# First attention: projection pieces two together in every second unit, in place of one in most units

## The chip, the cores and the metric

The kernel runs on one core of one Trainium2 chip. Time is the device time of one execution in microseconds (us); lower is better. A core has a tensor engine (PE, with its weight loads shown apart as PEld), VectorE (DVE), ScalarE (ACT), GpSimd (POOL) and a sync engine (SP) that here only issues transfers. Each runs its own program in order, and they meet through semaphores. Sixteen DMA engines serve the queues of SP, ACT and POOL.

## The reference

One decoder layer on 512 tokens of width 1024, float32. Two attentions read the same normalised input through one combined projection, their outputs are normalised, joined and projected, and an MLP follows:

```python
h = rms_norm(x, ln1_g[l])
proj = h @ w_in[l]
h_q, h_kv, h_kr, q_b, kv_b, gate_b = jnp.split(proj, offsets, axis=-1)
o_a = mla_mixer(h_q, h_kv, h_kr, ...)      # 8 heads, causal over 512 tokens
o_b = nsa_mixer(q_b, kv_b, gate_b, ...)    # 8 heads, 3 branches: compressed, selected, window
mix = jnp.concatenate([rms_norm(o_a, ...), rms_norm(o_b, ...)], axis=-1)
x = x + mix @ w_o[l]
h2 = rms_norm(x, ln2_g[l])
x = x + jnp.square(jax.nn.relu(h2 @ w_up[l])) @ w_down[l]
```

The change concerns how `kv_b`, the gates and the compressed branch's input (columns of `w_in` that only the second attention needs) are computed while the first attention runs.

## The kernel before

Tokens lie in 4 tiles `t` of 128. Weights are loaded in pieces of 128 x 1024 (`PIECES`) by SP into 3 raw slots. ACT rounds each piece to its high part (`split_hi`), DVE makes the rest (`split_lo`), and every product is made of three matmuls: high by high, low by high, high by low (`three`). A ring of 5 slots holds split pieces. SP issues the load of piece n when piece n - 3 has been split (`raw_free`).

The first attention (`mla`) is the list of the first 32 `UNITS`, one for each tile and head: unit n is tile n // 8, head n % 8. All engines walk through the units in one software pipeline, written out by hand. In step n PE does this, in this order: the scores of unit n; the projection pieces that `unit_of` puts there (`project`); the head transposes of steps 4 and 8 (`turn_heads`); the product with the values for unit n - 4 (from unit 16 on four units together); the transposes of the probabilities of unit n - 2 (`turn_unit`); and the transposes of a row whose norm was begun in step n - 4 (`turn_nsa`). In step n ACT copies out transposes of unit n - 3 (`pt_out`, the other ones are DVE's), makes the exponential of unit n - 1 (`exp_unit`), copies the keys of the second attention (`pair_his`), takes the squares of a row (`norm_in`), takes the gates and raw taps (`compress_in`) and splits weights. In step n DVE does `pt_out`, the mask and the maximum (`low_unit`), `pair_los`, `nsa_turned`, `nsa_row`, `nsa_sum`, `gate_row`, `out_row`, and the low halves of the pieces of step n - 1. POOL makes the powers of -1/2 in between, and issues one accumulating transfer behind each of them (`add_up`). Two PSUM banks each serve projections (`D`), transposes (`T`), scores (`S`) and outputs (`O`); a transpose waits until the one before the last has been copied out (`take`).

`ROWS` has 8 rows of projections for the second attention: `nkv` for tiles 0 to 3 (512 columns: keys and values of two branches), then `cmp` for tiles 0 to 3 (280 columns: compressed branch and gates). Each is 4 pieces of 6 matmuls. `ROW_END`, the step in which a row's last piece stands, sets when all that follows it is done:

```python
NORM_AT = {ROW_END[0]: ("nkv", 0), ROW_END[1]: ("nkv", 1), 9: ("nq", 3), ROW_END[2]: ("nkv", 2), ROW_END[3]: ("nkv", 3),
           16: ("nq", 2), 19: ("nq", 1), 22: ("nq", 0)}
PAIR_KEYS = {ROW_END[4 + t] + 1: t for t in range(NT)}
PAIR_LOWS = {n + int(t < NT - 1): t for n, t in PAIR_KEYS.items()}
```

A row in `NORM_AT` at step m has its squares (ACT) and sum (DVE) in step m + 1, its scaling (`nsa_row`, DVE) in step m + 3, its transposes (PE) in step m + 4 and their copy (`nsa_turned`, DVE) in step m + 5. `nq` rows are the queries of the second attention, whose projections were made earlier. The split of the pieces behind the `nkv` rows stands in steps 13 and 14, and that of output-projection piece `wo` 0 in step 17. The load of `wo` 0 waits for the low half of the second `cmp` piece, made by DVE in step 14.

Of the kernel before, what the change touches and what calls it, by code (L numbers as in the profile page):

```python
# [195 lines left out]


def unit_of(row, piece_):
    return 2 + (4 * row + piece_) * 27 // 32


ROW_END = [unit_of(r, 3) for r in range(len(ROWS))]

NORM_AT = {ROW_END[0]: ("nkv", 0), ROW_END[1]: ("nkv", 1), 9: ("nq", 3), ROW_END[2]: ("nkv", 2), ROW_END[3]: ("nkv", 3),
# [40 lines left out]
for _m, _n in enumerate(SPLITS[RING:]):  # L245
    _g = last_user(SPLITS[_m])
    _what = PIECES[_n][0]
    if _m + RING < BY_NAME:
        continue
    if _what == "wo":  # L250
        SPLIT_AT_UNIT.setdefault(N_MLA + WO_SPLIT[PIECES[_n][1]], []).append(_n)
    elif _g == ("wo", 0, NT - 1, 1):
        SPLIT_AT_UNIT.setdefault(N_MLA + 51, []).append(_n)
    elif _g == ("nkv", NT - 1):
        SPLIT_AT_UNIT.setdefault(1 + unit_of(ROWS.index(_g), PIECES[SPLITS[_m]][1]), []).append(_n)
    else:
        SPLIT_AFTER.setdefault(_g, []).append(_n)
# [76 lines left out]
def build(nc, a, out, known):  # L334
    with ExitStack() as ctx:
# [1793 lines left out]
        def _(pe):  # L2129
# [367 lines left out]
            for n in range(last + 10):  # L2497
# [6 lines left out]
                if n < N_MLA:  # L2504
                    for r, key in enumerate(ROWS):
                        here = [i for i in range(4) if unit_of(r, i) == n]
                        if here:
                            project(*key, here)
# [241 lines left out]
```

How the kernel before makes its waits and increments, by code:

```python
        @block.sync  # L712
# [5 lines left out]
                cols = slice(0 if i else 2 * P, D_MODEL)  # L718
                sp.dma_start(x_t[i][:, cols], a["x_t"][i, :, cols]).then_inc(*xt_in[i, part].mark())
            for n, (what, i, width, split) in enumerate(PIECES):
                for part, at_piece in X_LOADS.items():
                    if at_piece == n:
                        load_turned(*part)
                for t in ROWS_AT.get(n, ()):
                    load_x(t)
                if n >= RAW:
                    sp.wait_ge(*raw_free(n - RAW))
                if what == "quad" and n + 1 - RAW >= PIECE_AT["quad", (0, 0)]:
                    j = PIECES[n - RAW]
                    if j[0] == "quad":
                        sp.wait_ge(*dve_step.at(("w_diff", j[1][1])))
                if what == "sum" and PIECES[n - RAW][0] == "quad":
                    sp.wait_ge(*dve_step.at(("w_diff", PIECES[n - RAW][1][1])))
                if what == "sum":
                    k = SUM_JOBS.index(i)
                    sp.wait_ge(*sum_added[k % 4].at(k))
                    source = sums_dram[k]
                elif what in ("A", "B"):
                    k = 2 * i + int(what == "B")
                    sp.wait_ge(*up_added[k // BATCH].at(BATCH * (k // BATCH) + BATCH - 1))
                    source = up_sums[k]
                else:
                    source = a["w_pairs"][i, 0] if what == "P" else a["w_down"][i[0], i[1]] if what == "quad" else a["weights"][n, :, 0:width]
```

## Time and profile before

| | us |
|---|---|
| median of 3 runs (lowest, highest) | 633.57 (632.98, 635.29) |
| the profiled execution | 635.07 |
| its span in the trace | 633.2 |
| PE busy in the span | 621.1 |
| DVE busy | 499.6 |
| ACT busy | 399.5 |
| first attention, scores of units 0 to 31 | 92.5 to 169.5 |

Times in the trace count from the start of the span. A row of the timeline gives the start, the duration, the engine, the line of the kernel, what is written and read, and in brackets how long the engine was idle before and what released it. Matmuls are pipelined, so starts say more than durations.

### The profile page before, as it was taken

What the parts mean: (1) busy time and instruction counts of PE and PEld (TensorE: products, weight loads), DVE (VectorE), ACT (ScalarE), POOL (GpSimd) and SP (SyncE); (2) the same over time, 40 slices, a digit from 0 to 9 for tenths busy, and PEclk for the clock granted to TensorE, in tenths of its full rate; (3) what the DMA queues carried; (4) which work ended last, traced back from release to release, by engine and by line L of the source; (5) the groups of instructions that cost most, each with busy time, mean ns of one, the idle gap of its engine ahead of it and who ended that gap; (6) DMA issues with size and microseconds to landing.
All of it is one profiled execution on the core that took longest, in us unless ns stands there. A gap on an engine that the chain in (4) does not pass through costs nothing.

```text
span 633.2 us, 11668 instructions
## 1 busy us (share of the span) xinstructions
PE 621.1 (98%) x4105; PEld 550.9 (87%) x4105; DVE 499.6 (79%) x936; ACT 399.5 (63%) x800; POOL 161.0 (25%) x230
## 2 busy tenths in 40 slices
PE   7999999998999999999999999999999999999998
PEld 6999888887788888887899999999998888888886
DVE  6766666579988788897897787777778999998664
ACT  6584775657997647657458667676657464755660
POOL 0655655434332202212110111111111212222200
PEclk8999999999999999999999999999999999999999
DMA  8883528996999955996355878788877899899972
GB/s 325 290 320 129 203 108 325 294 298 184 256 271 295 356 184 171 293 257 145 68 135 184 224 212 226 203 202 234 182 169 168 230 230 251 217 247 283 282 252 100
DMA packets 34793, 142.48 MB, mean 225 GB/s; under 512 B 5319, under 2 KB 5831, under 8 KB 33776
## 3 DMA queue, kind: packets, MB, share of 16 engines
q1 hardware_dynamic: 22832, 83.66, 37.2%
q0 software_dynamic: 10208, 34.88, 30.1%
q10 hardware_dynamic: 1696, 23.21, 9.8%
q8 instruction: 33, 0.54, 0.3%
q14 instruction: 24, 0.20, 0.1%
HBM read 139.57 MB, written 65.06 MB: 323 GB/s over the span
## 4 chain that ended last, share of the span: by engine, by line
PE 89%; DVE 4%; ACT 3%; DMA 2%; issue 1%; POOL 0%; ACTq 0%; DVEq 0%; POOLq 0%
PE bank L2147 15%; PE bank L2149 15%; PE bank L2148 15%; PE bank L2556 7%; PE bank L2555 7%; PE bank L2554 7%; PE bank L2167 7%; PE bank L2392 3%; PE bank L2335 2%; PE bank L2374 2%; DMA raw<-weights 1%; PE bank L2346 1%; PE bank L2347 1%; PE bank L2490 1%; PE bank L2492 1%
## 5 line engine op out<-in xcount | busy, mean ns | idle before, releaser
L881 POOL DMA_DIRECT2D down_sums<-w_down x64 | 49.8, 779 | 229.0 <-PE bank L2556 137.0
L2147 PE MATMUL bank<-w_hi,act_hi 128*128 128x512 f32 (+3 forms) x222 | 88.7, 400 | 0.1
L2148 PE MATMUL bank<-w_lo,act_hi 128*128 128x512 f32 (+3 forms) x222 | 79.7, 359 | 0.0
L2149 PE MATMUL bank<-w_hi,act_lo 128*128 128x512 f32 (+3 forms) x222 | 79.7, 359 | 0.0
L1128 ACT ACTIVATE p_buf<-s_buf,stats 128x128 f32<-128x128 f32 (+3 forms) x96 | 53.8, 561 | 30.4 <-PE bank L2167 16.2
L1420 DVE TENSOR_TENSOR w_lo<-raw,w_hi 128x1024 fp32r<-128x1024 f32 (+1 forms) x50 | 60.0, 1207 | 15.1 <-ACT w_hi L987 14.7
L987 ACT ACTIVATE w_hi<-raw 128x1024 fp32r<-128x1024 f32 (+1 forms) x50 | 51.6, 1040 | 29.5 <-DMA raw<-w_pairs 21.8
L1370 ACT ACTIVATE w_hi<-raw 128x1024 fp32r<-128x1024 f32 x31 | 32.8, 1057 | 35.8 <-DMA raw<-down_sums 20.0
L2147 PE MATMUL bank<-w_hi,s_all 128*128 128x512 f32 x140 | 54.6, 390 | 0.0
L2148 PE MATMUL bank<-w_lo,s_all 128*128 128x512 f32 x140 | 54.5, 389 | 0.0
L2149 PE MATMUL bank<-w_hi,s_all 128*128 128x512 f32 x140 | 54.5, 389 | 0.0
L2147 PEld LDWEIGHTS bank<-w_hi,act_hi 128*128 128x128 f32 x222 | 42.3, 191 | 6.8 <-issue 1.4
L2554 PE MATMUL bank<-g_all,w_hi 128*128 128x256 f32 x168 | 47.5, 283 | 0.0
L2555 PE MATMUL bank<-g_all,w_hi 128*128 128x256 f32 x168 | 47.5, 283 | 0.0
L2556 PE MATMUL bank<-g_all,w_lo 128*128 128x256 f32 x168 | 47.5, 283 | 0.0
L2556 PE MATMUL bank<-act_hi,w_lo 128*128 128x256 f32 x168 | 47.5, 283 | 0.0
L2555 PE MATMUL bank<-act_lo,w_hi 128*128 128x256 f32 x168 | 47.5, 283 | 0.0
L2554 PE MATMUL bank<-act_hi,w_hi 128*128 128x256 f32 x168 | 47.5, 283 | 0.0
L2167 PE MATMUL bank<-consts,p_buf 128*128 128x128 f32 x248 | 45.1, 279 | 2.4 <-ACT pt_buf L1140 1.0
L2148 PEld LDWEIGHTS bank<-w_lo,act_hi 128*128 128x128 f32 x222 | 42.3, 191 | 5.9 <-issue 1.2
L2149 PEld LDWEIGHTS bank<-w_hi,act_lo 128*128 128x128 f32 x222 | 42.3, 190 | 5.4
L2028 DVE TENSOR_TENSOR w_lo<-raw,w_hi 128x1024 fp32r<-128x1024 f32 x31 | 37.8, 1219 | 11.3 <-ACT w_hi L1370 11.1
(329 smaller groups left out, 1832.0 us busy)
## 6 DMA issues: line engine op xcount, KB each, us to landing
down_sums<-w_down ACTq DMA_DIRECT2D x32, 512.0 KB, 6.4
down_sums<-w_down POOLq DMA_DIRECT2D x64, 256.0 KB, 5.7
raw<-down_sums SPq DMA_DIRECT2D x32, 512.0 KB, 4.9
up_sums<-w_pairs POOLq DMA_DIRECT2D x28, 512.0 KB, 9.8
raw<-up_sums SPq DMA_DIRECT2D x28, 512.0 KB, 4.8
raw<-weights SPq DMA_DIRECT2D x26, 512.0 KB, 5.8
up_sums<-w_pairs SPq DMA_DIRECT2D x16, 512.0 KB, 6.3
raw<-w_down SPq DMA_DIRECT2D x16, 512.0 KB, 5.3
```

The costliest lines, as they stand in the source:

```text
L881: pool.dma_start(sums_dram[k, rows_], a["w_down"][SUMS[m][1], step, rows_], accum_op=ALU.add, max_dma_last_dim=4096).then_inc(*sum_added[k ...
L987: ins = act.activation(hi[:, 0:width], raw[:, n % RAW, 0:width], ACT.Copy)
L1128: act.activation(p_buf[:, n % 2, 0:nk], s_buf[:, n % 2, 0:nk], ACT.Exp, scale=-1.0, bias=neg_max[:, m:m + 1], accum_out=den[:, d:d + 1]).t ...
L1420: ins = dve.tensor_tensor(lo[:, 0:width], raw[:, n % RAW, 0:width], hi[:, 0:width].bitcast(F32), ALU.subtract)
L2028: dve.tensor_tensor(lo, src, hi.bitcast(F32), ALU.subtract).then_inc(*lo_done.mark(JOBS[d]))
L2147: pe.matmul(dst, a_h, w_h, start=start, stop=False, skip_group_check=onto)
L2148: pe.matmul(dst, a_h, w_l, start=False, stop=False, skip_group_check=onto)
L2149: return pe.matmul(dst, a_l, w_h, start=False, stop=stop, skip_group_check=onto)
L2167: ins = pe.transpose(bank[0:m, i * step:i * step + k], tile, ident[0:k, 0:k])
L2554: pe.matmul(dst, h[:, k * P:(k + 1) * P], g_h[:, k, :], start=start and k == 0, stop=False, skip_group_check=onto)
L2555: pe.matmul(dst, h[:, k * P:(k + 1) * P], g_l[:, k, :], start=False, stop=False, skip_group_check=onto)
L2556: ins = pe.matmul(dst, l[:, k * P:(k + 1) * P], g_h[:, k, :], start=False, stop=k == KD // 2 - 1, skip_group_check=onto)
```

## The change

The function that places piece `piece_` of row `row` in a step is changed. Nothing else is edited:

```diff
 def unit_of(row, piece_):
-    return 2 + (4 * row + piece_) * 27 // 32
+    return 2 + (4 * row + piece_) // 2 * 27 // 16
```

Steps of the four pieces of each row, before and after:

| row | before | after |
|---|---|---|
| nkv 0 | 2 2 3 4 | 2 2 3 3 |
| nkv 1 | 5 6 7 7 | 5 5 7 7 |
| nkv 2 | 8 9 10 11 | 8 8 10 10 |
| nkv 3 | 12 12 13 14 | 12 12 13 13 |
| cmp 0 | 15 16 17 18 | 15 15 17 17 |
| cmp 1 | 18 19 20 21 | 18 18 20 20 |
| cmp 2 | 22 23 23 24 | 22 22 23 23 |
| cmp 3 | 25 26 27 28 | 25 25 27 27 |

`ROW_END` goes from 4, 7, 11, 14, 18, 21, 24, 28 to 3, 7, 10, 13, 17, 20, 23, 27, and with it the steps that are derived from it. The steps in which weights are split stay where they are.

## Rows read from the trace of the kernel before

**Rows 1.** The page: busy time of each engine, and the chain's shares

```profile
PE 621.1 (98%) x4105; PEld 550.9 (87%) x4105; DVE 499.6 (79%) x936; ACT 399.5 (63%) x800; POOL 161.0 (25%) x230
...
PE 89%; DVE 4%; ACT 3%; DMA 2%; issue 1%; POOL 0%; ACTq 0%; DVEq 0%; POOLq 0%
```

**Rows 2.** Waits of PE, 92 to 185 us: total, times, longest

```profile
PE bank L2167 <- DVE pt_buf L1615: 1.6, 1, 1.6
PE bank L2167 <- ACT pt_buf L1140: 1.0, 1, 1.0
```

**Rows 3.** Windows: busy time by engine, then PE's granted clock and DMA

```profile
4.00:8.00 4.00, 2.15 (x8) 0.95 (x6) 1.89 (x5) 2.53 (x6) 0.00 (x0) 1.00 1.04 400
8.00:12.00 4.00, 4.00 (x15) 3.93 (x14) 4.00 (x9) 4.00 (x9) 0.00 (x0) 0.57 1.00 378
...
139.00:144.00 5.00, 2.82 (x20) 2.21 (x18) 4.20 (x10) 4.93 (x15) 0.00 (x0) 1.00 1.03 264
```

**Rows 4.** Timeline of PE, steps 7 and 8

```profile
106.87 0.39 PE L2147 MATMUL bank<-w_hi,act_hi 128*128 128x512 f32 x1
...
108.23 0.33 PE L2374 MATMUL bank<-m_v,pt_buf 128*128 128x64 f32 x2
108.39 0.28 PE L2167 MATMUL bank<-consts,p_buf 128*128 128x128 f32 x1
...
112.20 0.41 PE L2167 MATMUL bank<-consts,o_nsa 128*128 128x128 f32 x2 [0.18 <-ACT m_k L1077]
```

**Rows 5.** Timeline of DVE, 102 to 109 us

```profile
102.14 0.42 DVE L1553 TENSOR_TENSOR qk_row<-kr,stats 128x256 f32<-128x256 f32 x1
...
104.14 0.41 DVE L1661 TENSOR_REDUCE stats<-square 128x4 f32<-128x256 f32 x1
...
108.50 0.43 DVE L1679 TENSOR_TENSOR raw_row<-raw_row,stats 128x256 f32<-128x256 f32 x1 [2.52 <-POOL stats L786]
```

**Rows 6.** Timeline of DVE and SP, steps 14 and 15

```profile
126.82 0.68 DVE L1704 COPY n_q<-bank 128x512 f32<-128x512 f32 x1
...
128.21 1.76 DVE L1417 SCALAR_TENSOR_TENSOR w_lo<-raw,stats,w_hi 128x280 fp32r<-128x280 f32 x4
...
129.16 0.33 SPq L745 DMA_DIRECT2D raw<-weights  x1
```

**Rows 7.** Timeline of ACT, DVE and PE, steps 17 to 20

```profile
138.08 0.72 ACT L977 ACTIVATE w_hi<-raw,consts 128x512 fp32r<-128x512 f32 x1 [4.02 <-DMA raw<-weights]
...
139.44 1.42 DVE L1409 SCALAR_TENSOR_TENSOR w_lo<-raw,consts,w_hi 128x512 fp32r<-128x512 f32 x2 [3.47 <-ACT w_hi L977]
...
140.88 1.70 ACT L1184 ACTIVATE act_hi<-n_k 64x256 fp32r<-64x256 f32 x4
...
141.59 0.68 DVE L1675 TENSOR_TENSOR nq_row<-n_q,stats 128x512 f32<-128x512 f32 x1
...
144.36 0.63 PE L2167 MATMUL bank<-consts,o_nsa 128*128 128x128 f32 x4 [1.55 <-DVE pt_buf L1615]
144.59 1.72 DVE L1723 TENSOR_TENSOR act_lo<-n_k,act_hi 64x256 fp32r<-64x256 f32 x4
```

**Rows 8.** Timeline of DVE and PE, the last two query rows

```profile
150.25 0.69 DVE L1690 TENSOR_TENSOR o_nsa<-nq_row,consts 128x512 f32<-128x512 f32 x1
...
152.74 0.60 PE L2167 MATMUL bank<-consts,o_nsa 128*128 128x128 f32 x4
...
157.55 0.69 DVE L1690 TENSOR_TENSOR o_nsa<-nq_row,consts 128x512 f32<-128x512 f32 x1
...
159.34 0.63 PE L2167 MATMUL bank<-consts,o_nsa 128*128 128x128 f32 x4
```

**Rows 9.** Transfers: size and time to landing; issued at 129.16, at 140.89, whole page

```profile
raw<-weights SPq DMA_DIRECT2D x1, 512.0 KB, 8.9
...
raw<-weights SPq DMA_DIRECT2D x1, 512.0 KB, 8.1
...
raw<-weights SPq DMA_DIRECT2D x26, 512.0 KB, 5.8
```

## The prediction

> **What bounds the kernel now.** I read four views. First the page's shares: the tensor engine (PE) is busy for 98% of the span, and 89% of the chain that ended last is PE's [rows 1]. So every microsecond for which PE stands still, and does not stand still now, is added to the time, and the change can give back only what PE waits for now. Second the waits of PE in the stretch of the first attention (92 to 185 us): one of 1.6 us and one of 1.0 us, and little beside them [rows 2]. Third the timeline there, engine by engine. Those two waits have one root: ScalarE (ACT) stood 4.02 us for the load of the first output-projection piece, wo 0, and everything that it and VectorE (DVE) had queued behind that came late [rows 7]. Fourth the windows: in 139 to 144 us PE is busy for 2.82 of 5 us, its lowest share of the stage [rows 3]. So the stage holds about 2.6 us that a better order could win, and PE is otherwise its own bound.
>
> **The change.** Nothing is removed or added: the 32 pieces (8 rows of 4) are issued with the same matmuls. A piece of the first four rows costs 108.23 - 106.87 = 1.36 us of PE [rows 4]; one of the last four is 280 columns wide in place of 512, so about 0.75 us. The number of units with pieces falls from 27 to 16. Matmul time is the same sum, so this part costs 0; what changes is who waits.
>
> Three things move. (a) PE gets 11 units without a piece, which are short. (b) Rows 0, 2 to 7 end one unit earlier (ROW_END is 3, 7, 10, 13, 17, 20, 23, 27 in place of 4, 7, 11, 14, 18, 21, 24, 28). All that NORM_AT, PAIR_KEYS and PAIR_LOWS derive from it moves too: ACT's squares and key copies, DVE's sums, normalised rows and gates, GpSimd's (POOL's) powers with the accumulating transfer issued behind each, and PE's transposes of keys. (c) The queries' steps at 9, 16, 19, 22 stand still, so they meet other neighbours. PAIR_LOWS becomes 19, 22, 25, 28 in place of 20, 23, 26, 29: DVE's pair_los now runs in just the units 19, 22, 25 in which it makes the normalised query rows, and ahead of them in its program. Splits keep their units. I follow the waits in order.
>
> *Unit 3.* Its second piece needs the low half that DVE makes from 97.4 us; PE reaches it some 0.3 us early and then has nothing more than before to do. About 0.2 us, inside what follows.
>
> *Unit 7, the transposes of key row 0.* Before they ran at 112.20, in unit 8. Now they stand in unit 7 behind the transpose of 108.39 [rows 4], so PE wants them at 108.5. They need the row that DVE made from 108.50, behind POOL's power, for which it waited 2.52 us [rows 5]: two steps of 0.42 us, so 109.3. That is a wait of 0.8 us even if nothing else moves. But DVE's sum of that row (0.41 us at 104.14) now stands ahead of the head rows that began at 102.14, and has to wait there for ACT's squares; I put that at 0.9 us, and POOL's chain follows the head rows. So the wait is 1.8 us. About 0.4 us of waiting at the old place goes. Net +1.4 us from here on, bounds 0.8 and 1.9.
>
> *Unit 14.* Key row 2 is now transposed one unit behind query row 3. With the transposes' two banks used in turn it needs that row's bank, and DVE copied it out only from 126.82 for 0.68 us [rows 6], in step 14. PE has about 1 us of work between the two, since unit 14 has no piece, while DVE's mask step and this copy take 0.5 + 0.68 us behind the transposes and the copy of another. About +0.7 us, bounds 0 and 1.1.
>
> *The wo 0 load.* SP may issue it when DVE has made the low half of piece 1 of row 4: 128.21 plus half of the group of 1.76 us, and SP issues at 129.16 [rows 6]. DVE reaches that work only after the copy of query row 3. That row's transposes come 1.4 us late by unit 7, and one piece (1.36) later since unit 13 holds two pieces in place of one: 2.8 us. In front of the split DVE has no longer a normalised key row (0.8) but the sum of key row 3 (0.33). So the load is issued 2.8 - 0.5 = 2.3 us late, at 131.5. The wait of unit 14 runs beside this and isn't added.
>
> It landed 8.9 us after its issue, and the next such load 8.1 [rows 9]. I take 8.1, since POOL's transfer of 123.62 will be 2 us older by then: it lands at 139.6, 1.5 us later than 138.1. ACT wants it at 136.1, so the wait stays about as long and comes later. The page DMA: Bandwidth & Descriptors of the Trainium skill (Queues, rings and completion order) says that each engine takes the queues that have work in turn, packet by packet. By that rule the landing depends on how many other transfers are in flight, which no row here separates.
>
> *From the landing to query row 2's transposes (unit 20).* Before this took 144.36 - 138.05 = 6.3 us [rows 7]: query row 2 was scaled on DVE from 141.59, ahead of ACT's gates and of pair_los (144.59, 1.72). Now the gates of tile 0 and its key copies fall to unit 18. In ACT's program the key copies (1.70) come before the gate step (0.9 to its end), so ACT needs 1.24 (split, 138.08 to the exponential) + 0.6 (exponential) + 1.7 + 0.9 = 4.4 us [rows 7]. DVE stands at the gates for that long, with the low half of wo 0 behind them. Then it has gates 0.4, wo 0's low half 1.35 (1.42 as shown, less the overlap), a mask step 0.5, pair_los 1.75, the query row 1.3, and the copy of the 17th unit's transpose 0.4, whose bank PE needs: 5.7 us. Together 10.1, with 0.1 for the signal 10.2 us: 3.9 us more than now. One piece of 0.8 us that PE had still to do before is done by then. Delay of PE at this point: 2.3 - 0.8 (the shorter landing) + 3.9 - 0.8 = **+4.6 us**. This holds the waits of units 7 and 14, which lie earlier on the same chain; PE itself would have been there 3 to 4 us sooner and stands in front of unit 20's transposes.
>
> *Query rows 1 and 0 (units 23 and 26).* Row 1 was scaled at 150.94 (150.25 + 0.69) and transposed at 152.74: 1.8 us of slack [rows 8]. pair_los takes 1.75 of it, and the gates behind ACT's copies some more: +0.6, bounds 0 and 1. Row 0 was scaled at 158.24 and transposed at 159.34: 1.1 us of slack. Units 24 to 26 hold one piece less than before (0.8 us), and pair_los takes 1.75: 1.1 - 0.8 - 1.75 = -1.4, so **+1.4**, bounds 0 and 1.9.
>
> *After that* PE's work is the same. Its later waits on others add up to about a microsecond up to 330 us, so little can be absorbed.
>
> Sum: 4.6 + 0.6 + 1.4 = 6.6 us. The profiled execution took 635.07 us around a span of 633.2; the sum is made on its span. The median of the runs shown is 633.57, and a difference carries over: 633.57 + 6.6 = **640.2 us**, +1.0%.
>
> **Rivals.** *The load lands as loads usually do.* The page's median for a weight load is 5.8 us [rows 9]. Then it lands 3.1 us sooner than with 8.9, unit 20 is delayed by 2.3 - 3.1 + 3.9 - 0.8 = 2.3 us, and the time is 633.57 + 2.3 + 2.0 = 637.9. For it: POOL's transfer of key row 2 is older. Against: the three neighbours of this load were no quicker than 8.1.
>
> *Not slower, the other side.* If the load lands within 4.6 us, before ACT asks for it at 136.1, the root of both waits of [rows 2] is gone: -2.6 us, 631.0 us. This decides only if DVE is by then not behind, so that pair_los in front of the query rows is hidden as well. The quickest loads of 512 KB on the page have a median of 4.8, in a later stage.
>
> *No difference.* The short units and the long ones even out; DVE's moved steps stay covered and only unit 7's wait is left: 633.57 + 1.4 = 635.0. For it: DVE is idle for a fifth of the whole span [rows 1]. Against: that idle time lies elsewhere than in units 18 to 26.
>
> *The clock falls as well.* PE stands 3 to 4 us in front of unit 20's transposes. Where PE was busy for 2.15 of 4 us, the next 4 us show a granted clock of 0.57, near the lower of its two levels (1.2 and 2.4 GHz); with 2.82 busy of 5 us it stayed at 1.00 [rows 3]. If it falls here, some 4 us run at half speed: +2 us, 642.2. The page TensorE: Matmul & The Clock Gate of the Trainium skill (HAM oscillation) says that gaps of a few microseconds between groups of matmuls bring the clock down each time; the rows of this stage don't show it so far.
>
> **How the numbers follow.** Forecast 0.55; usual landing 0.20; clock 0.10; no difference 0.09; other side 0.06. The first three are slower by over 0.5% (3.2 us, about what a measurement of this kernel can tell from no change): 0.85. Within it 0.09, faster 0.06. Low bound: the usual landing with the query rows' waits at 0 gives 635.9, and half of the no-difference case is let in: 635.2. High bound: landing 8.9 (+0.8), query rows at their bounds (+0.9), 641.9, with most of the clock's 2 us: 643.5.
>
> **What would show it.** Right: a new wait of PE at 108 to 111 us for DVE's key row; the SP issue of wo 0 at 131 to 132; PE waiting 3 us or more for the query row of unit 20 around 146 to 150, with DVE busy without a break; the start of the second attention some 6 us later, and no difference after it. Wrong: wo 0 landing before 137; DVE idle in front of the query rows; PE waits of under 3 us in all in the stretch.

## The result, and the profile after

The changed kernel took 642.99 us (median of 4 runs, 641.73 to 643.94), the kernel before beside it 633.78 (median of 4). The ratio is 1.014, with a 95% interval of 1.011 to 1.017: slower by 9.2 us, 2.6 us more than the forecast's sum and inside its range. The profiled execution took 643.94 us around a span of 642.1, which is 8.9 us more than the span before. That difference is accounted for below.

The page after, busy time and the shares of the chain that ended last:

```profile
PE 625.0 (97%) x4105; PEld 552.6 (86%) x4105; DVE 500.1 (78%) x936; ACT 399.6 (62%) x800; POOL 161.0 (25%) x230
...
PE 84%; DVE 6%; ACT 4%; DMA 3%; issue 2%; POOL 1%; ACTq 0%; DVEq 0%; POOLq 0%
```

Against [rows 1] the 8.9 us fall into two parts. PE's idle time went from 633.2 - 621.1 = 12.1 to 642.1 - 625.0 = 17.1 us: 5.0 us more standing. Its busy time went up by 3.9 us with the same 4105 matmuls. Two falls of PE's clock, shown below, make about 3.1 of it; the remaining 0.8 us isn't traced to a place (the trace with only the first pair_los late, in which the clock doesn't fall, has 1.0 us more than before as well). The share of DVE, ACT and DMA in the chain grew from 9% to 13%.

PE's waits after, 92 to 195 us (total, times, longest), where before had 1.6 and 1.0 [rows 2]:

```profile
PE bank L2167 <- DVE pt_buf L1615: 2.0, 1, 2.0
PE bank L2167 <- DVE o_nsa L1690: 1.6, 1, 1.6
PE bank L2167 <- DVE o_nsa L1694: 1.3, 1, 1.3
PE bank L2335 <- DVE stats L1603: 1.0, 2, 0.8
PE bank L2167 <- ACT p_buf L1128: 1.0, 1, 1.0
PE bank L2167 <- DVE n_q L1704: 0.6, 1, 0.6
```

Behind 190 us PE's waits are the same in both traces (0.8, 0.4 and 0.4 us), so all of it happens under the first attention. The timeline of PE shows where:

```profile
110.47 0.44 PE L2167 MATMUL bank<-consts,o_nsa 128*128 128x128 f32 x2 [1.30 <-DVE o_nsa L1694]
116.17 0.60 PE L2335 MATMUL bank<-m_k,m_q 96*128 96x256 f32 x2
...
130.64 0.41 PE L2167 MATMUL bank<-consts,o_nsa 128*128 128x128 f32 x2 [0.60 <-DVE n_q L1704]
...
146.77 0.63 PE L2167 MATMUL bank<-consts,o_nsa 128*128 128x128 f32 x4 [1.97 <-DVE pt_buf L1615]
...
148.99 1.01 PE L2147 MATMUL bank<-w_hi,act_hi 128*128 128x280 f32 x1
...
156.92 1.02 PE L2335 MATMUL bank<-m_k,m_q 96*128 96x512 f32 x2
163.96 0.66 PE L2167 MATMUL bank<-consts,o_nsa 128*128 128x128 f32 x4 [1.63 <-DVE o_nsa L1690]
173.98 0.66 PE L2167 MATMUL bank<-consts,p_buf 128*128 128x128 f32 x4 [1.00 <-ACT p_buf L1128]
175.40 2.05 PE L2335 MATMUL bank<-m_k,m_q 96*128 96x512 f32 x2 [0.76 <-DVE stats L1603]
...
180.40 0.47 PE L2346 MATMUL bank<-act_hi,q_pairs 128*128 128x512 f32 x1
```

The same instructions before, as far as they aren't shown above:

```profile
114.55 0.60 PE L2335 MATMUL bank<-m_k,m_q 96*128 96x256 f32 x2
153.18 1.02 PE L2335 MATMUL bank<-m_k,m_q 96*128 96x512 f32 x2
168.60 1.02 PE L2335 MATMUL bank<-m_k,m_q 96*128 96x512 f32 x2
171.87 0.47 PE L2346 MATMUL bank<-act_hi,q_pairs 128*128 128x512 f32 x1
```

Read against these, with 0.78 us (a late piece) taken off where the new order has done one piece more by then:

| place | before | after | delay |
|---|---|---|---|
| score of unit 10 | 114.55 | 116.17 | 1.6 |
| query row 2 (unit 20) | 144.36 | 146.77 | 1.6 |
| score of unit 24 | 153.18 | 156.92 | 3.0 |
| query row 0 (unit 26) | 159.34 | 163.96 | 4.6 |
| score of unit 31 | 168.60 | 175.40 | 6.8 |
| second attention starts | 171.87 | 180.40 | 8.5 |

The delay grows at five places: unit 7, between units 20 and 24, unit 26, units 28 to 31, and from there to the second attention. The second and the last of them hold a fall of PE's clock. The windows (busy time by engine, then PE's granted clock, DMA share, GB/s):

```profile
144.00:148.00 4.00, 2.03 (x15) 1.50 (x13) 3.62 (x8) 1.69 (x5) 0.20 (x1) 1.00 1.10 338
148.00:152.00 4.00, 4.00 (x18) 3.39 (x17) 2.93 (x9) 3.01 (x9) 2.52 (x2) 0.57 0.66 207
172.00:176.00 4.00, 2.23 (x9) 1.04 (x8) 3.90 (x12) 3.01 (x8) 0.00 (x0) 0.93 0.49 153
176.00:180.00 4.00, 4.00 (x35) 2.45 (x33) 1.63 (x5) 1.37 (x5) 2.49 (x8) 0.64 0.77 261
```

PE worked 2.03 and 2.23 of 4 us, and in the next 4 us the granted clock was 0.57 and 0.64, near the lower of its two levels (1.2 of 2.4 GHz). Before, every such window from 140 to 184 us shows 1.00. Twelve matmuls of a `cmp` unit took 148.99 to 152.01 = 3.0 us; the twelve of two units before, at 1.00, took 142.45 to 144.31 = 1.9. The Trainium skill, in TensorE: Matmul & The Clock Gate (A second HAM failure mode: psum-queue depth-cycling), says that small idle times between groups of matmuls can be enough to bring the clock down again and again. This trace agrees, with waits of 1.97 us in one case and of 1.00 and 0.76 in the other; the last section has traces in which waits as long did not.

PE waits for DVE in all of these but one (ACT's `p_buf`, 1.00 us). DVE's timeline after:

```profile
109.53 0.42 DVE L1679 TENSOR_TENSOR raw_row<-raw_row,stats 128x256 f32<-128x256 f32 x1 [3.53 <-POOL stats L786]
...
140.85 0.18 DVE L1710 TENSOR_SCALAR gates<-gates 128x24 f32<-128x24 f32 x1 [1.31 <-ACT gates L1149]
...
141.28 1.31 DVE L1409 SCALAR_TENSOR_TENSOR w_lo<-raw,consts,w_hi 128x512 fp32r<-128x512 f32 x2
...
142.99 1.72 DVE L1723 TENSOR_TENSOR act_lo<-n_k,act_hi 64x256 fp32r<-64x256 f32 x4
144.74 0.69 DVE L1675 TENSOR_TENSOR nq_row<-n_q,stats 128x512 f32<-128x512 f32 x1
145.47 0.69 DVE L1690 TENSOR_TENSOR o_nsa<-nq_row,consts 128x512 f32<-128x512 f32 x1
146.07 0.55 DVE L1615 COPY pt_buf<-bank 128x384 f32<-128x384 f32 x1
...
160.74 1.72 DVE L1723 TENSOR_TENSOR act_lo<-n_k,act_hi 64x256 fp32r<-64x256 f32 x4
162.49 0.69 DVE L1675 TENSOR_TENSOR nq_row<-n_q,stats 128x512 f32<-128x512 f32 x1
163.21 0.69 DVE L1690 TENSOR_TENSOR o_nsa<-nq_row,consts 128x512 f32<-128x512 f32 x1
...
171.23 1.72 DVE L1723 TENSOR_TENSOR act_lo<-n_k,act_hi 64x256 fp32r<-64x256 f32 x4 [0.56 <-ACT act_hi L1184]
172.99 0.18 DVE L1710 TENSOR_SCALAR gates<-gates 128x24 f32<-128x24 f32 x1
...
174.65 0.68 DVE L1603 CUSTOM_DVE_ANT_0 s_buf<-bank,consts 128x512 f32<-128x512 f32 x1
```

From 140.85 to 146.6 DVE works without a break: gates, the low half of `wo` 0, a mask, pair_los, the query row, and only then the copy that releases PE's bank. In step 25 pair_los (1.72 us) stands straight in front of query row 0, and in unit 26 PE waits 1.63 us for that row. In step 28 pair_los stands in front of the gates, the split of a `wo` piece and the mask step of unit 29 (174.65), for which PE waits 0.76 us at the score of unit 31. The wait of 1.00 us just before is not DVE's. It is for ACT's exponential of unit 28, which stands behind the key copies and the gates of step 28:

```profile
170.37 0.83 ACT L1184 ACTIVATE act_hi<-n_k 64x256 fp32r<-64x256 f32 x2
...
171.22 0.84 ACT L1184 ACTIVATE act_hi<-n_k 64x256 fp32r<-64x256 f32 x2
...
173.10 0.73 ACT L1128 ACTIVATE p_buf<-s_buf,stats 128x512 f32<-128x512 f32 x1
```

ACT and the transfer of `wo` 0 went otherwise than forecast. SP issued the load at 131.68, as predicted (131.5), but it landed in 4.3 us, not 8.1, and ACT took it at once:

```profile
136.35 1.32 ACT L977 ACTIVATE w_hi<-raw,consts 128x512 fp32r<-128x512 f32 x2
...
138.45 0.83 ACT L1184 ACTIVATE act_hi<-n_k 64x256 fp32r<-64x256 f32 x2
...
139.31 0.84 ACT L1184 ACTIVATE act_hi<-n_k 64x256 fp32r<-64x256 f32 x2
...
140.54 0.27 ACT L1149 ACTIVATE gates<-bank,stats 128x24 f32<-128x24 f32 x1
```

Where before stands a wait of 4.02 us [rows 7], there is none. DVE's gates wait (1.31 us, to 140.85) has another cause: ACT's key copies, 1.7 us, stand in front of the gate step, as the forecast had it.

### The profile page after: what moved, and what is told of

It is laid out like the page before. It is cut to its first block, busy times and chain, and to the rows that moved or that the text cites. A ratio compares the mean times of both kernels' runs of the same rounds, so it can differ in the third digit from the quotient of the medians.

```text
span 642.1 us, 11668 instructions
## 1 busy us (share of the span) xinstructions
PE 625.0 (97%) x4105; PEld 552.6 (86%) x4105; DVE 500.1 (78%) x936; ACT 399.6 (62%) x800; POOL 161.0 (25%) x230
## 4 chain that ended last, share of the span: by engine, by line
PE 84%; DVE 6%; ACT 4%; DMA 3%; issue 2%; POOL 1%; ACTq 0%; DVEq 0%; POOLq 0%
PE bank L2147 15%; PE bank L2149 15%; PE bank L2148 15%; PE bank L2167 7%; PE bank L2554 6%; PE bank L2556 6%; PE bank L2555 6%; PE bank L2392 3%; PE bank L2374 2%; PE bank L2335 2%; PE bank L2346 1%; PE bank L2347 1%; DMA raw<-up_sums 1%; DVE w_lo L1420 1%; PE bank L2490 1%
## 5 line engine op out<-in xcount | busy, mean ns | idle before, releaser
L2147 PE MATMUL bank<-w_hi,act_hi 128*128 128x512 f32 (+3 forms) x222 | 86.7, 391 | 0.2
```

The costliest lines, as they stand in the source:

```text
L2147: pe.matmul(dst, a_h, w_h, start=start, stop=False, skip_group_check=onto)
```

## The experiments

The change has two sides: pieces in pairs, and everything that ROW_END carries along (the "followers"). The first four kernels part the two; the next ones part the followers; the last ones test the clock and the order in the kernel before. All ratios are to the kernel before, timed beside them. Where a gain is given against the change, it is a difference of medians taken at different times; the kernel before had medians of 633.8 to 635.2 us beside them, so about 1 us of such a gain is not to be told from nothing.

**Pairs alone.** The changed kernel, with the followers where they were:

```diff
-ROW_END = [unit_of(r, 3) for r in range(len(ROWS))]
+ROW_END = [4, 7, 11, 14, 18, 21, 24, 28]
```

> The pieces stand as in the changed kernel, two together, but ROW_END is written out as 4, 7, 11, 14, 18, 21, 24, 28, so that norms, key copies, gates and pair_los stay in the steps of before. Theory A (the cost comes from what moved along with ROW_END): 634 us, between 633 and 637; no PE wait for key row 0 at unit 7, none for query rows 2, 1 and 0 of over 1.6 us, clock at 1.00 through 146 to 180 us. Rival B (steps without a piece are too short to cover the softmax chain, wherever the norms stand): 640 us or more.

635.84 us, ratio 1.0024 (1.0002 to 1.0047): +1.4 us of the change's 9.2. The span was 634.5 us, PE's longest wait 0.5 us, and the clock 1.00 throughout. Pairing is nearly free. The interval reaches from 0.1 to 3.0 us, and the stage itself is only 0.3 us longer in the trace (see the table at the end of this section).

**Followers alone.** The kernel before, with the changed ROW_END:

```diff
+ROW_END = [3, 7, 10, 13, 17, 20, 23, 27]
```

> The pieces stand one in most units as before, but ROW_END is written out as 3, 7, 10, 13, 17, 20, 23, 27, so that only the norms, key copies, gates and pair_los move. Theory A: slower like the changed kernel, 639 to 644 us. Rival B: 633 to 635 us, since no unit is left without a piece that had one.

647.14 us, ratio 1.0196 (1.0135 to 1.0257): +12.7 us, more than the whole change. The load of `wo` 0 was issued at the same time (131.62) but took 6.7 us, ACT waited 2.1 us for it, and PE:

```profile
PE bank L2167 <- DVE pt_buf L1615: 4.4, 1, 4.4
PE bank L2167 <- DVE o_nsa L1690: 3.3, 2, 2.3
PE bank L2167 <- DVE o_nsa L1694: 1.2, 1, 1.2
```

The waits for the query rows are there, larger than in the change (this trace is of an execution of 649.61 us, 2.5 us above the median). So the followers make the loss; with the pieces in pairs less of it shows. The two parts don't add up (1.4 + 12.7 against 9.2).

**Norms early, keys and gates late; and the other way round.** Only the first half of ROW_END is moved, then only the second:

```diff
+ROW_END = [3, 7, 10, 13, 18, 21, 24, 28]    # first
+ROW_END = [4, 7, 11, 14, 17, 20, 23, 27]    # second
```

> The changed kernel with only the last four entries of ROW_END put back (18, 21, 24, 28): the norms of the key rows stay early, the key copies, gates and pair_los go back to their steps. Theory A with the size split as the trace of the changed kernel shows it: the wait at unit 7 (1.6 us) stays, what comes from unit 20 on goes: 635.5 us, between 634.5 and 637. Rival B: 640 or more.

> The changed kernel with only the first four entries of ROW_END put back (4, 7, 11, 14): the norms of the key rows go back, the key copies, gates and pair_los stay early. Theory A: the wait at unit 7 goes, those from unit 23 on stay: 640 to 642 us. Rival B: 641 or more, no different from the changed kernel by over 1 us.

The first took 636.33 us, ratio 1.0041 (1.0018 to 1.0064); the second 642.73, ratio 1.0132 (1.0106 to 1.0158). The waits of units 7 and 14 (1.3 and 0.6 us) are in the first trace, yet its span is no longer than with pairs alone (634.2 against 634.5). Its first attention began 0.85 us sooner, though. From the first score to the start of the second attention it took 80.1 us, pairs alone 79.6: 0.5 us for 1.9 us of waits. Most of them is made good later, and pairs alone has small waits of its own in units 8 to 16 (0.51 us for `w_lo`, 0.25 and 0.23 us for copies) that are missing here. The second has all of the change's loss, with o_nsa 1.7, pt_buf 1.6, stats 1.0 and p_buf 1.0 us. The loss sits in what follows the `cmp` rows.

**pair_los one step later.** That leaves key copies with pair_los, and gates. First pair_los alone is put back to steps 20, 23, 26 and 29, behind the query rows:

```diff
-PAIR_LOWS = {n + int(t < NT - 1): t for n, t in PAIR_KEYS.items()}
+PAIR_LOWS = {n + 1 + int(t < NT - 1): t for n, t in PAIR_KEYS.items()}
```

> The changed kernel with only pair_los put back to units 20, 23, 26 and 29, behind the query rows of units 19, 22 and 25; key copies on ScalarE and gates stay early. Theory C (the 1.72 us of pair_los in front of each query row are the bulk): 637 to 639.5 us. Rival D (VectorE stands at the gates until ScalarE has done its key copies; that is the bulk): 641 us or more.

637.56 us, ratio 1.007 (1.0046 to 1.0095): 5.4 us of the loss gone. Query row 2's transposes start at 144.54 with a wait of 0.24 us, in place of 146.77 and 1.97, no o_nsa L1690 wait is left, and the clock is 1.00 throughout.

**Gates late; keys late.** A second list, CMP_END = [18, 21, 24, 28], is used in place of ROW_END's second half, first for `compress_in` and `gate_row` alone, then for PAIR_KEYS (and so pair_los) alone:

```diff
-                    gate_row(ROW_END.index(n - 1) - NT)
+                    gate_row(CMP_END.index(n - 1))
...
-PAIR_KEYS = {ROW_END[4 + t] + 1: t for t in range(NT)}
+PAIR_KEYS = {CMP_END[t] + 1: t for t in range(NT)}
```

> The changed kernel with only compress_in (ScalarE) and gate_row (VectorE) put back to the steps after 18, 21, 24 and 28; key copies and pair_los stay early. Theory C: 641 us or more. Rival D: 637 to 639.5 us.

> The changed kernel with the key copies and pair_los put back and only the gates early. Theory C: 637 us, as with norms early and all four entries of keys and gates late (636.3). Rival D: between 636.3 and 638, since with no key copies ahead of it the gate step is soon done; so this run tells only whether gates alone cost anything: over 638.5 would go against both.

Gates late: 639.28 us, ratio 1.0089 (1.006 to 1.0118), 3.7 us of the loss gone; the wait at unit 20 is down to 1.4 us and that for query row 0 to 0.7. In its trace the clock stays at 1.00 behind unit 20 and falls only in 172 to 176 us (0.65). Keys late: 635.03 us, ratio 1.0015 (0.9999 to 1.003), 8 us of it gone. PE is busy for the full 4 us of each of these windows at clock 1.00:

```profile
144.00:148.00 4.00, 4.00 (x28) 3.42 (x27) 3.86 (x14) 3.56 (x11) 1.41 (x2) 1.00 1.01 325
148.00:152.00 4.00, 4.00 (x43) 3.40 (x41) 3.90 (x11) 2.91 (x7) 1.32 (x2) 1.00 0.83 212
```

The gates cost something only if the key copies stand in front of them: early gates with late keys are free. The effects overlap: pair_los late and gates late give 5.4 + 3.7 = 9.1 us, while the change is only 7.2 us above pairs alone, which has all of them late.

**One pair_los at a time.** Only the last (28 to 29), then only the first (19 to 20):

```diff
+PAIR_LOWS = {n + 1: t for n, t in PAIR_KEYS.items()}                               # only the last
+PAIR_LOWS = {n + int(t < NT - 1) + int(t == 0): t for n, t in PAIR_KEYS.items()}   # only the first
```

> The changed kernel with only the last pair_los (tile 3) put back to unit 29. If the waits of units 28 to 31 (1.0 us for ScalarE's exponential, 0.76 for the mask step) come from it, with the second fall of the clock behind them: 3 to 4 us less than the changed kernel, 639 to 640 us. If they come from the short unit 28: 642 or more.

> The changed kernel with only the first pair_los (tile 0) put back to unit 20. If it makes the 1.97 us wait of unit 20 and with it the first fall of the clock: 3 to 3.5 us less than the changed kernel, 639.5 to 640 us. If the gates are what counts there: less than 1 us less, 642 or more.

Only the last: 642.12 us, ratio 1.0118 (1.0088 to 1.0149), a gain of about 1 us, and 2.4 us of span. My theory that pair_los makes the waits of units 28 to 31 fell. They are still there without it. PE waits as long for ACT's exponential of unit 28, which stands behind the key copies, and DVE's mask step of unit 29 is still late, since DVE waits for ACT's gates, which ACT does behind its key copies too:

```profile
172.49 0.18 DVE L1710 TENSOR_SCALAR gates<-gates 128x24 f32<-128x24 f32 x1 [2.10 <-ACT gates L1149]
```

PE waits 1.00 and 0.55 us there, in place of 1.00 and 0.76, and now the clock of 176 to 180 us stays at 1.00. Only the first: 639.43 us, ratio 1.008 (1.005 to 1.011), 3.6 us gained. Query row 2's transposes start at 144.97, 1.8 us sooner: one pair_los. The clock stays at 1.00 from 140 to 180 us, with the waits of units 28 to 31 as long as they were (1.0 and 1.0 in sum).

**The wait filled with work.** To see what the first fall of the clock costs, PE makes 14 matmuls in the wait of unit 20; their results are thrown away:

```diff
+                if n == 20:
+                    pe.wait_ge(*copied.at(("cmp", 0)))
+                    for _ in range(14):
+                        pe.matmul(D[known["bank", "D", ("cmp", 0)]][:, 0:256], act_hi[:, 0, 0:P], act_hi[:, 0, 0:256], start=True, stop=True)
```

> The changed kernel with 14 extra matmuls of 256 columns into a projection bank that nobody reads, in PE's program just ahead of query row 2's transposes in unit 20, where PE waits 1.97 us. They take some 1.6 to 1.8 us of PE's program and are thrown away. If PE's standing idle there is what brings the granted clock down in 148 to 152 us (0.57 in the changed kernel, which I put at 1.7 us): 1.00 there, and 641.3 us. If the clock falls for another reason, 0.57 stays and the time is 643 us or a little more.

642.43 us, ratio 1.013 (1.0102 to 1.0157), not to be told from the change. The fall is gone: the filler ran for 1.92 us, PE then waited 0.48, and the next window reads

```profile
148.00:152.00 4.00, 4.00 (x26) 3.32 (x25) 2.66 (x9) 3.65 (x12) 2.73 (x3) 1.00 0.48 161
```

in place of 0.57. So in these two traces the clock fell where PE stood still and kept up where work stood in its place. By the transposes of query row 1 PE is 0.97 us ahead of the change, though it was 0.26 behind at unit 20, and waited 0.21 for that row:

```profile
155.52 0.66 PE L2167 MATMUL bank<-consts,o_nsa 128*128 128x128 f32 x4 [0.21 <-DVE o_nsa L1690]
163.19 0.66 PE L2167 MATMUL bank<-consts,o_nsa 128*128 128x128 f32 x4 [1.48 <-DVE o_nsa L1690]
...
174.64 1.12 PE L2335 MATMUL bank<-m_k,m_q 96*128 96x512 f32 x2 [0.77 <-DVE stats L1603]
```

0.97 + 0.26 + 0.21 = 1.44 us: that is what the first fall cost, as the table above has it (3.0 - 1.6 = 1.4). About half of it came back: 0.77 us at query row 0, 0.76 at the score of unit 31. The rest went to the filler, which ran a little over the wait, and to waits for DVE, which made the row at the same time as in the change (start 154.77 against 154.51). The second fall still came (0.60 in 176 to 180 us), behind the same waits of units 28 to 31.

**In the kernel before: `wo` 0 later, query row 2 later.** The kernel before has its own wait for this load, so I tried to take it away, by a split one step later, or by the query row one step later:

```diff
+WO_SPLIT = {0: 18 - N_MLA, 1: 27 - N_MLA, 2: 9, 3: 26, 4: 31, 5: 33, 6: 35, 7: 39}   # first
+           17: ("nq", 2), 19: ("nq", 1), 22: ("nq", 0)}                              # second
```

> The kernel before with the split of output-projection piece 0 in step 18 in place of 17, so that ScalarE makes the exponential of unit 17 before it stands for the load. If the two waits of 1.0 and 1.6 us are the load's alone: 632 us, 1 to 2.5 us faster than before. If they come from what ScalarE and VectorE have queued in steps 19 and 20 anyway: 634, no difference.

> The kernel before with query row 2's norm in step 17 in place of 16, so that its scaling leaves VectorE's step 19, in which the low half of the output-projection piece comes late, and its transposes stand in unit 21. If the 1.6 us wait for the copy of unit 17's transposes is made by that scaling: 632 to 633 us, 0.5 to 1.5 us faster than before. If the gates and the load alone make it: no difference.

The first: 634.15 us (median without the profiled execution), ratio 1.0006 (0.9982 to 1.0029): nothing gained. Its profiled execution ran at a mean clock of 0.56 (1016 us) and can't be read, so where the wait went stays open. The second: 638.0 us, ratio 1.0037 (1.0012 to 1.0062), slower. ACT still waited 3.57 us for the load, and the later row made PE wait 2.5 us for o_nsa in a stretch in which the clock fell to 0.66. No kernel here beat the one before; of those with the pieces in pairs, early gates with late keys came nearest.

The traces side by side. The stage is counted from the score of unit 0 to the first score of the second attention, the last stretch from the score of unit 31 on:

| kernel | stage, us | last stretch, us |
|---|---|---|
| before | 79.4 | 3.3 |
| the change | 87.7 | 5.0 |
| pairs alone | 79.6 | 3.3 |
| followers alone | 91.1 | 3.4 |
| norms early, keys and gates late | 80.1 | 3.3 |
| norms late, keys and gates early | 86.3 | 3.4 |
| pair_los late | 81.7 | 3.4 |
| gates late | 84.3 | 5.0 |
| keys late, gates early | 78.9 | 3.4 |
| last pair_los late | 85.9 | 3.4 |
| first pair_los late | 83.8 | 3.4 |
| wait filled | 86.9 | 5.0 |
| before, query row 2 later | 82.0 | 3.3 |

The last stretch holds the same matmuls each time, and takes 5.0 us only in the three traces in which the clock is down in it. With norms late PE had the same waits of 1.00 and 0.77 us in units 28 to 31 as in the change, with the clock at 1.00. So the second fall costs 1.6 us by itself. Executions of one kernel seem to differ in this: the change's four had a mean clock of 0.992, 0.997, 0.992 and 0.994, and the one at 0.997 took 641.73 us, 2.2 us less than the profiled one (0.992).

## Why the prediction was right, and where its sum was not

The direction and the mechanism (DVE's and ACT's steps moved in front of the query rows) held. That the size came out is luck, as the sum at the end shows. Taken one by one:

- *Matmul time costs 0; pairing is only a matter of who waits.* Pairs alone cost 1.4 us (0.1 to 3.0); in the trace 0.3 us of it lies in the stage, and where the rest lies is open.
- *Unit 7, +1.4.* Measured 1.6 by the score of unit 10, with a wait of 1.30 us where 1.8 was put. DVE's row started at 109.53, 1.03 late. But the step took this delay as lasting to the end of the chain, and with norms early the stage is only 0.5 us longer than with pairs alone: most of it was swallowed later.
- *Unit 14, +0.7, not added.* Measured 0.60.
- *Load of `wo` 0 issued at 131.5.* Measured 131.68.
- *It lands 8.1 us after its issue, at 139.6.* This step failed: 4.3 us, at 136.0. I took the duration of the load issued at 140.89, under other traffic (see the last section).
- *Query row 2 delayed by 4.6.* Mis-sized by that: 1.6. The chain of DVE behind the gates was right (from gates at 140.85 to the copy's end 5.8 us, forecast 5.7), and ACT's order too; only their start, which hung on the load, was put 3.1 us too late (139.6 + 4.4 = 144.0).
- *Query row 1, +0.6.* Measured as a wait: 0, since the slow clock had by then made PE late by 1.4 us; with the wait of unit 20 filled it is 0.2 us.
- *Query row 0, +1.4.* Measured 1.6 (a wait of 1.63 us).
- *After that nothing.* This step failed: units 28 to 31 gave 2.2 us (6.8 - 4.6), in waits of 1.00 and 0.76 us. They are the fourth repeat of the same pattern (ACT's key copies in front of its exponential and of the gates, and behind the gates a split in front of DVE's mask step), which I worked out only for the three query rows.
- *The clock rival, 0.10, +2 at unit 20.* It came true at unit 20 (+1.4) and again at 176 us (8.5 - 6.8 = +1.7). The rows pointed both ways: behind 2.15 of 4 us busy the clock had fallen, behind 2.27 of 4 us (140 to 144 us before) it had not.
- *The rival of the usual landing (637.9).* It had this load nearer: it put unit 20 at +2.3, where 1.6 was measured. It missed the time because it, too, had nothing for units 28 to 31 and for the clock.
- *The signs.* One sign of being right failed (PE waiting 3 us or more for the query row of unit 20: 1.97 us), and one of being wrong came true (`wo` 0 landing before 137). The others held: the issue at 131.68, the wait at 110.47 for the key row, DVE busy without a break, and the delay of the second attention, 8.5 us where some 6 were put.
- *The other side.* Its condition, the load within 4.6 us, was met, and the time was 9 us longer. It named its own way out: DVE was behind by then, and pair_los in front of the query rows was not hidden.

So the sum of 6.6 came near the 8.9 of the span by luck, because errors of both signs met: -3.0 at unit 20 and -0.6 at query row 1, against +0.2 at query row 0, +2.2 in units 28 to 31 and +3.1 of clock; that makes 8.5, and the last 0.4 lie behind 180 us. Of the cause this is shown: the key copies and pair_los one step earlier carry most of the loss (ratio 1.0015 with them put back, 1.014 without). Open remains what made one 512 KB load take 8.9 us and the other 4.3 (the last section has what fits), and why the clock falls behind the same waits in one execution and not in another. The kernel with the last pair_los late got rid of the second fall in its trace and is 2.4 us shorter there, but its median is only about 1 us lower, within the intervals.

## What to carry to other kernels

When a step of an in-order pipeline is moved, follow every list that is derived from its number; here the pieces themselves cost 0.2%, and two 1.7 us steps that slid ahead of results that PE needed (DVE's pair_los, and ACT's key copies ahead of its gates and exponential) cost most of the rest. Work such a pattern out for each of its repeats up to the end of the stage, not only for those where a known consumer stands. And a PE wait removed is worth its length only if the engine that it waited for is not late again one unit on.

## What the runs showed of the hardware

A later issue landed sooner. The `wo` 0 load, 512 KB each time, took 8.9 and 7.9 us when issued at 129.16 (before, and query row 2 later). Issued between 130.67 and 132.47, in the eleven traces that hold some part of the change, it took 4.2 to 6.7 us and landed between 134.9 and 138.3. The traces show what else was in flight. In the first 4.2 us behind the issue, before and after:

```profile
q10 hardware_dynamic: 41, 0.85, 51.4%
q10 hardware_dynamic: 17, 0.03, 2.1%
```

q10 carries ACT's transfers (packets, MB, share of the 16 engines). Before, ACT had issued one of 512 KB at 125.82, which took 9.1 us, and another at 130.40, just behind the load; in the change its transfers were issued at 128.97 and 133.79, around the load. Over all 13 readable traces the load's time follows this traffic roughly: 8.9 and 7.9 us beside 0.85 and 0.79 MB, 6.7 beside 0.39, 4.7 to 5.5 beside 0.16 to 0.36, and 4.2 to 4.3 beside 0.13 MB or less. That is a correlation; no run moved ACT's transfers alone, and the next SP loads, issued 0.8 to 2.4 us behind, moved too. The Trainium skill, in DMA: Bandwidth & Descriptors (Queues, rings and completion order), says that an engine takes the queues that have work in turn. A load that has to share its engines with ACT's queue would fit that.

The clock fell behind some of PE's waits and not behind others of the same length:

| trace | waits of PE, us | PE busy of 4 us | clock there, and in the next 4 us |
|---|---|---|---|
| the change, 144 to 148 | 1.97 | 2.03 | 1.00, 0.57 |
| the change, 172 to 176 | 1.00 and 0.76 | 2.23 | 0.93, 0.64 |
| norms late, 172 to 176 | 1.00 and 0.77 | 2.23 | 1.00, 1.00 |
| norms late, 144 to 148 | 0.85 and 1.40 | 2.32 | 0.79, 0.78 |
| before, 140 to 144 | 0.98 and 1.55 | 2.27 | 1.00, 1.00 |
| gates late, 144 to 148 | 1.41 | 2.59 | 1.00, 1.00 |

So neither the length of the waits nor PE's busy time in such a window tells a fall from none here. What does is open.
